# The gated delta rule's 64x64 triangular matrices, stored packed with two heads a tile and multiplied in the diagonal quarters of TensorE's array

## The chip, the core and the metric

The kernel runs on one core of one Trainium2 chip. The metric is the device time of the whole program in microseconds, here the median of three runs. A profile is taken of one further execution.

## What is computed

Two networks in a row on a sequence of 512 tokens, width 1024: a first one of two layers (a recurrent and gated-linear-attention mixer, then an attention with forgetting, called fox, each with an MLP) and a second one of two *hybrid* layers. A hybrid layer mixes with three things at once: sliding-window attention, sparse attention, and the gated delta rule. The change concerns the delta rule alone, four heads of width 128, chunks of 64 tokens:

```
q, k, v, g, beta = ...                       # per head; gc = cumsum(g) within a chunk of 64
decay = where(lower, exp(gc[:, None] - gc[None, :]), 0)
a_mat = where(strict, (k * beta) @ k.T * decay, 0)          # 64x64 for each chunk
rhs   = [v * beta, k * beta * exp(gc)]
u, w  = triangular_solve(a_mat + I, rhs)                    # unit lower triangular
qk    = where(lower, q @ k.T * decay, 0)                    # 64x64 for each chunk
for each chunk:                                             # 8 chunks, a scan
    v_new = u - w @ state
    o     = (q * exp(gc)) @ state + qk @ v_new
    state = state * exp(gc_last) + (k * exp(gc_last - gc)).T @ v_new
```

All arithmetic is float32.

## The kernel before

The program is written for the engines by hand, each engine with its own order of instructions and semaphores by name (`ev.mark` and `ev.at`). In a hybrid layer the attention and the delta rule share one stage. `paired_attention` goes through 34 slots `d`. In each it issues the two score products of slot d (L763, 64 contraction rows, one head in each row half), then the first delta step (`fill(d, 0)`), the products with the values of slot d-2 (L774, the two heads into the two column halves of a bank), the first transpose of the probabilities of slot d-1 (L788), the second delta step (`fill(d, 1)`) and the second transpose. VectorE takes the maxima (L1339), scales (L1362) and copies half the transposes (L1369); ScalarE takes the exponentials (L1916) and copies the other half (L1927). `STEPS` lays the list of `delta_steps` over the slots, two a slot, from slot 1 on.

The list has, for each pair of heads (0, 1) and (2, 3): rows, tok, kk of each head, then xt; then for each level k of 1 to 4 the step p for both heads and q for one and for the other; then p of level 5, last, and uw of each head. These are 23 steps for a pair. After both pairs come 16 steps of the scan over chunks (scan, kv).

The inverse of the unit triangular matrix is built by levels: X is the inverse so far, of blocks of 2^k, `XTM` its transpose, and `ATL` the transposed a_mat. A level takes the mask of its off-diagonal blocks (`level`, VectorE), p is their product with X (TensorE, L1007), ScalarE copies it to `PM` (L2190), q multiplies it with X from both sides (L1015 for X, L1018 for its transpose), and VectorE subtracts (L1630, L1632). The next p waits for the updates of the level before.

Each of these matrices stands in a tile of 128x512: 4 blocks of 128 tokens, each block a 128x128 matrix with two 64x64 chunks on its diagonal and zeros elsewhere. A product is a 128x128x128 product for each block. Each head of a pair has its own tiles, `gw(e, n)`, in `work_2` and `work`, and its own two banks, `ga(h)` and `gb_(h)`. `rows` broadcasts gc and a factor of beta over the partitions by a product with the identity (L971, L972), VectorE adds the mask of the decay (L1591) and multiplies k with beta (L1595), ScalarE takes the exponentials (L2170, L2171); `tok` transposes k and v (L982); `kk` forms k k^T and k q^T (L990, L991); `xt` transposes (L997); `uw` forms u and w (L1031, L1032). In the scan, chunk c of `qk` is read from rows and columns of its own 64x64 block (L1058).

The constants (masks, identity and tables) come in one DMA at the start, and TensorE waits for them before its first product.

## Time and profile before

| what | value |
|---|---|
| median of 3 runs | 3070.65 us (3068.67 to 3077.63) |
| the profiled execution's own time | 3068.48 us |
| its span on the core | 3067.0 us |
| mean granted TensorE clock | 0.956 of full (2.4 GHz) |
| TensorE, VectorE, ScalarE busy | 94%, 55%, 37% of the span |

Times in rows are microseconds from the start of the span; ns where it says so. PE is TensorE's products, PEld its weight loads, DVE VectorE, ACT ScalarE. The shapes of a product are its weights (rows*columns) and what it moves through them. The duration shown for one product contains its way through the array, so products overlap, and the pitch from start to start tells what one costs. A float32 product leaves two records. The granted clock is a share of 2.4 GHz: 1.00 is 2.4 GHz, 0.50 is 1.2 GHz.

### The profile page before, as it was taken

The page shows a single profiled execution, that of the slowest core. Times are in us where ns is not written, and L with a number is a line of the kernel's source. Part 1 is how long each engine was busy: PE and PEld are TensorE (multiplying, and loading weights), DVE is VectorE, ACT ScalarE, POOL GpSimd, SP SyncE. Part 2 cuts the span into 40 slices and gives each one's busy share as a digit, 9 for nine tenths or more (in the row PEclk, how much of TensorE's full clock was granted, in tenths as well). Part 3 has the DMA queues.
Part 4 walks back from the last instruction along what each step waited for, and adds up shares of the span by engine and source line. Part 5 has one row for each costly group of instructions (what it writes and reads, how often), then busy time and mean ns, then how long its engine had stood idle before and what let it go on. Part 6 is the DMA issues. An engine that isn't in the chain of part 4 may idle for free.

```text
span 3067.0 us, 35358 instructions
## 1 busy us (share of the span) xinstructions
PE 2870.2 (94%) x14106; PEld 2297.8 (75%) x14106; DVE 1673.6 (55%) x2910; ACT 1121.2 (37%) x1908; POOL 9.4 (0%) x21
## 2 busy tenths in 40 slices
PE   6878999999998999997998989999999999899998
PEld 4666888867666688884887767888868778678887
DVE  6748756563555665655546755444555477543334
ACT  3433423234554432424424443222334344332223
POOL 0000000000000000000000000000000000000000
PEclk9969999999998999998988999999999899999999
DMA  6324655532221365661230003444432100122222
GB/s 237 130 69 151 199 188 169 190 116 86 72 67 49 108 203 183 193 205 62 96 103 1 1 28 107 140 145 144 147 110 96 70 1 2 55 86 99 97 97 83
DMA packets 92067, 336.19 MB, mean 110 GB/s; under 512 B 10480, under 2 KB 10736, under 8 KB 91776
## 3 DMA queue, kind: packets, MB, share of 16 engines
q1 hardware_dynamic: 86800, 315.40, 31.1%
q10 hardware_dynamic: 3792, 14.31, 1.3%
q0 software_dynamic: 1312, 4.23, 0.5%
q8 instruction: 113, 1.85, 0.2%
q14 instruction: 50, 0.41, 0.0%
HBM read 331.76 MB, written 2.13 MB: 109 GB/s over the span
## 4 chain that ended last, share of the span: by engine, by line
PE 87%; DVE 7%; ACT 4%; DMA 1%; issue 1%; ACTq 0%; DVEq 0%
PE bank L595 22%; PE bank L596 22%; PE bank L597 22%; PE bank L774 2%; PE bank L788 2%; PE bank L763 2%; DVE in_low L1175 1%; DVE hidden L1178 1%; PE bank L1007 1%; PE bank L862 1%; PE bank L612 1%; PE bank L1015 1%; PE bank L613 1%; PE bank L614 1%; PE bank L643 1%
## 5 line engine op out<-in xcount | busy, mean ns | idle before, releaser
L595 PE MATMUL bank<-in_high,weights_high 128*128 128x512 f32 x2160 | 874.0, 405 | 45.8 <-DVE in_low L1175 34.5
L596 PE MATMUL bank<-in_low,weights_high 128*128 128x512 f32 x2160 | 856.0, 396 | 0.0
L597 PE MATMUL bank<-in_high,weights_low 128*128 128x512 f32 x2160 | 855.5, 396 | 0.0
L1085 DVE TENSOR_TENSOR weights_low<-weight_ring,weights_high 128x1024 fp32r<-128x1024 f32 x404 | 494.0, 1223 | 467.0 <-ACT weights_high L1710 467.0
L1710 ACT ACTIVATE weights_high<-weight_ring 128x1024 fp32r<-128x1024 f32 x404 | 424.6, 1051 | 482.7 <-PE bank L597 320.6
L595 PEld LDWEIGHTS bank<-in_high,weights_high 128*128 128x128 f32 x2160 | 414.3, 192 | 183.0 <-issue 55.4
L597 PEld LDWEIGHTS bank<-in_high,weights_low 128*128 128x128 f32 x2160 | 414.3, 192 | 88.9
L596 PEld LDWEIGHTS bank<-in_low,weights_high 128*128 128x128 f32 x2160 | 415.2, 192 | 85.3 <-issue 3.8
L595 PE MATMUL bank<-hidden_split,weights_high 128*128 128x512 f32 x864 | 336.2, 389 | 0.0
L597 PE MATMUL bank<-hidden_split,weights_low 128*128 128x512 f32 x864 | 336.2, 389 | 0.0
L596 PE MATMUL bank<-hidden_split,weights_high 128*128 128x512 f32 x864 | 336.2, 389 | 0.0
L1094 DVE CUSTOM_DVE_ANT_0 weight_ring<-weight_ring,silu_c,vectors 128x1024 f32<-128x1024 f32 x192 | 244.5, 1279 | 4.3 <-DMA weight_ring<-stream 4.2
L595 PEld LDWEIGHTS bank<-hidden_split,weights_high 128*128 128x128 f32 x864 | 162.2, 188 | 33.8
L597 PEld LDWEIGHTS bank<-hidden_split,weights_low 128*128 128x128 f32 x864 | 162.2, 188 | 33.7
L596 PEld LDWEIGHTS bank<-hidden_split,weights_high 128*128 128x128 f32 x864 | 162.2, 188 | 33.5
L1803 ACT ACTIVATE hidden_split<-tmp 128x512 fp32r<-128x512 f32 x108 | 68.4, 633 | 262.6 <-DVE tmp L1539 205.5
L1724 ACT ACTIVATE tmp<-bank 128x512 f32<-128x512 f32 (+1 forms) x77 | 45.9, 596 | 243.9 <-PE bank L597 243.9
L1916 ACT ACTIVATE probs<-probs,columns 128x256 f32<-128x256 f32 (+4 forms) x144 | 73.5, 512 | 165.5 <-DVE columns L1339 163.2
L1195 DVE TENSOR_TENSOR hidden_split<-tmp,hidden_split 128x512 fp32r<-128x512 f32 x108 | 74.8, 693 | 75.5 <-ACT hidden_split L1803 75.5
L1539 DVE TENSOR_TENSOR tmp<-bank,tmp 128x512 f32<-128x512 f32 x44 | 30.4, 691 | 118.3 <-PE bank L597 118.3
L1724 ACT ACTIVATE tmp<-bank,vectors 128x512 f32<-128x512 f32 (+1 forms) x65 | 44.6, 686 | 136.7 <-PE bank L597 136.7
L774 PE MATMUL bank<-probs_T,hidden 128*64 128x128 f32 (+1 forms) x816 | 70.6, 299 | 25.1 <-DVE probs_T L1369 25.1
(330 smaller groups left out, 2985.8 us busy)
## 6 DMA issues: line engine op xcount, KB each, us to landing
weight_ring<-stream SPq DMA_DIRECT2D x597, 512.0 KB, 3.4
mixer_out<-cmp ACTq DMA_DIRECT2D x6, 1024.0 KB, 4.8
hidden<-forget_rows POOLq DMA_DIRECT2D x16, 256.0 KB, 3.6
residual<-x ACTq DMA_DIRECT2D x4, 512.0 KB, 12.9
mixer_out<-cmp SPq DMA_DIRECT2D x2, 1024.0 KB, 5.9
out<-mixer_out ACTq DMA_DIRECT2D x4, 512.0 KB, 2.7
constants<-consts ACTq DMA_DIRECT2D x1, 2013.5 KB, 20.9
silu_c<-c ACTq DMA_DIRECT2D x2, 512.0 KB, 4.6
```

Source lines behind the costliest of these rows:

```text
L595: pe.matmul(bank[:, :], WHI[:, z, cols], high, start=(k == 0), stop=False)
L596: pe.matmul(bank[:, :], WHI[:, z, cols], low, start=False, stop=False)
L597: ins = pe.matmul(bank[:, :], WLO[:, z, cols], high, start=False, stop=(k == ktiles - 1))
L763: pe.matmul(B[2 + z][:, 0:w], it["q"], it["k"], start=True, stop=True).then_inc(*mark("tensor_attention", *name, "scores", 2 * d + z))
L774: ins = pe.matmul(it["out"], it["v"][c], turned[:, blk(c)], start=it["start"] and c == 0, stop=it["stop"] and c == m - 1, skip_group_check ...
L1085: v.tensor_tensor(WLO[:, z, :], ring[:, n % RING, :], WHI[:, z, :].bitcast(F32), ALU.subtract).then_inc(*mark("weights_low", "low", n))
L1094: v.tensor_tensor_reduce(w, w, SC[:, :], 1.0, vec1("ada_b", col, col + 1), ALU.mult, ALU.add, MODS[:, col:col + 1]).then_inc(*mark("modula ...
L1195: v.tensor_tensor(HSPLIT[:, 1, at_, :], tmp, HSPLIT[:, 0, at_, :].bitcast(F32), ALU.subtract).then_inc(*mark("vector_mlp", *event))
L1710: s.activation(WHI[:, i % NSPLIT, :], ring[:, n % RING, :], ACT.Copy).then_inc(*mark("weights_high", "high", n))
L1724: s.activation(dst, view(B_of(key)[:, :]), func, **kw).then_inc(*mark("scalar_evict", "evicted", key))
L1803: s.activation(HSPLIT[:, 0, at_, :], tmp, ACT.Copy).then_inc(*mark("scalar_mlp", *event))
L1916: s.activation(p, p, ACT.Exp, bias=nm, scale=-1.0, accum_out=COL[:, c + 2 + z:c + 3 + z]).then_inc(*mark(sem, *name, "exp", i))
```

## The change

- All 64x64 matrices are stored without their zeros. A packed matrix is 128 partitions x 256 columns: chunk 2b in partitions 0 to 63 and chunk 2b+1 in 64 to 127, both at columns 64b. Both heads of a pair share a tile of 512 columns (`pk(e, n)`), so operations that take a tile and a constant (level masks, the start of the inverse) run once for both heads, 512 wide. The others run once for each head, 256 wide.
- The products of xt, p, q and last are 64x64x64, two for each of before. Chunk z of a block is multiplied in the quarter of rows and columns of half z (`out64`, `half`), and successive products alternate between the two diagonal quarters, with different heads or different results, and so different banks. xt is a product with a 64x64 identity instead of a transpose.
- kk forms 128x64x64 products into both column halves.
- In rows, the broadcast of gc stays whole for the exponential `EG`; that of beta and a second one of gc are made packed. beta is multiplied onto the decay matrix (`PMB`) after its exponential, no longer onto k; tok waits for that.
- uw becomes two steps for the pair: step 0 takes chunk 0 of each block for u and chunk 1 for w, step 1 the other way round.
- p and last signal once for both heads. The mask for the next level waits for p of the level before.
- The scan reads `qk` at its packed place. The constants shrink: decay mask and identity 64 columns, six level masks 64 columns each, no `strict`.

The number of steps and their places in the slots stay. The core of the diff:

```diff
-                 ("rot", 128), ("band", 128), ("causal", 128), ("decay_mask", 128), ("strict", 128),
-                 ("levels", 6 * 128), ("gla_mask", 64), ("chunk_reset", T), ("cos", T), ("sin", T),
+                 ("rot", 128), ("band", 128), ("causal", 128), ("decay_mask", 64), ("ident64", 64),
+                 ("levels", 6 * 64), ("gla_mask", 64), ("chunk_reset", T), ("cos", T), ("sin", T),
...
-    level_mask = lambda e, k: M[:, 4 + 2 * e + k % 2, :]
+    pk = lambda e, n: U2[:, n, 256 * e:256 * e + 256]
+    pkb = lambda e, n, z, b: U2[half(z), n, 256 * e + 64 * b:256 * e + 64 * b + 64]
+    level_pair = lambda k: M[:, 4 + k % 2, :]
+    level_block = lambda e, k, z, b: M[half(z), 4 + k % 2, 256 * e + 64 * b:256 * e + 64 * b + 64]
+    out64 = lambda bank, z, b: bank[half(z), 64 * b:64 * b + 64]
...
-            out += [("p", hs, 5), ("last", hs)] + [("uw", h) for h in hs]
+            out += [("p", hs, 5), ("last", hs), ("uw", hs, 0), ("uw", hs, 1)]
...
-                    ins = pe.matmul(gb_(h)[:, blk(b)], c4(brow)[:, b, h:h + 1].broadcast_to([P, P]), ident,
-                                    start=True, stop=True)
+                for n, x in enumerate((brow, crow)):
+                    for b in range(NTB):
+                        for z in range(2):
+                            ins = pe.matmul(out64(gb_(h), z, NTB * n + b), c4(x)[:, b, h:h + 1].broadcast_to([P, 64]),
+                                            ident[:, half(z)], start=True, stop=True)
...
-                pe.wait_ge(*at("gdn_kbt", l, h))
+                pe.wait_ge(*at("gdn_pmb", l, h))
...
-                for b in range(NTB):
-                    pe.matmul(ga(h)[:, blk(b)], H[:, 4 + h, blk(b)], gw(e, KBT)[:, blk(b)], start=True, stop=True)
-                    ins = pe.matmul(gb_(h)[:, blk(b)], H[:, 4 + h, blk(b)], H[:, h, blk(b)], start=True, stop=True)
+                for bank, src in ((ga(h), 4 + h), (gb_(h), h)):
+                    for b in range(NTB):
+                        for z in range(2):
+                            ins = pe.matmul(out64(bank, z, b), H[:, 4 + h, chunk(2 * b + z)], H[:, src, chunk(2 * b + z)],
+                                            start=True, stop=True)
...
             elif name == "p":
                 hs, k = which
-                for e, h in enumerate(hs):
-                    pe.wait_ge(*at("gdn_mask", l, h, k))
+                pe.wait_ge(*at("gdn_mask", l, hs, k))
+                for h in hs:
                     pe.wait_ge(*at("gdn_xm", l, h, k))
                     if k > 1:
                         pe.wait_ge(*at("gdn_xtm_k", l, h, k - 1))
+                for turn_ in range(2):
                     for b in range(NTB):
-                        ins = pe.matmul(gb_(h)[:, blk(b)], level_mask(e, k)[:, blk(b)], gw(e, XM)[:, blk(b)],
-                                        start=True, stop=True)
-                    ins.then_inc(*mark("tensor_gdn", "gdn_p", l, h, k))
+                        for e, h in enumerate(hs):
+                            z = turn_ ^ e
+                            ins = pe.matmul(out64(gb_(h), z, b), level_block(e, k, z, b), pkb(e, XM, z, b),
+                                            start=True, stop=True)
+                ins.then_inc(*mark("tensor_gdn", "gdn_p", l, hs, k))
             elif name == "q":
...
-                for b in range(NTB):
-                    ins = pe.matmul(ga(h)[:, blk(b)], gw(e, XTM)[:, blk(b)], gw(e, PM)[:, blk(b)], start=True, stop=True)
+                for turn_ in range(2):
+                    for b in range(NTB):
+                        z = turn_
+                        pe.matmul(out64(ga(h), z, b), pkb(e, XTM, z, b), pkb(e, PM, z, b), start=True, stop=True)
+                        z = 1 - turn_
+                        ins = pe.matmul(out64(gb_(h), z, b), pkb(e, PM, z, b), pkb(e, XTM, z, b), start=True, stop=True)
...
             elif name == "uw":
-                h, = which
-                e = h % 2
-                pe.wait_ge(*at("gdn_xtm_k", l, h, 5))
-                for b in range(NTB):
-                    pe.matmul(ga(h)[:, blk(b)], gw(e, XTM)[:, blk(b)], gw(e, VBT)[:, blk(b)], start=True, stop=True)
-                    ins = pe.matmul(gb_(h)[:, blk(b)], gw(e, KBG)[:, blk(b)], gw(e, XTM)[:, blk(b)], start=True, stop=True)
-                ins.then_inc(*mark("tensor_gdn", "gdn_uwt", l, h))
+
+                hs, turn_ = which
+                for e, h in enumerate(hs):
+                    if turn_ == 0:
+                        pe.wait_ge(*at("gdn_xtm_k", l, h, 5))
+                    else:
+                        pe.wait_ge(*at("gdn_uw_half", l, h))
+                    for b in range(NTB):
+                        z = turn_
+                        pe.matmul(ga(h)[half(z), blk(b)], pkb(e, XTM, z, b), gw(e, VBT)[half(z), blk(b)], start=True, stop=True)
+                        z = 1 - turn_
+                        ins = pe.matmul(gb_(h)[:, chunk(2 * b + z)], gw(e, KBG)[half(z), blk(b)], pkb(e, XTM, z, b),
+                                        start=True, stop=True)
+                    ins.then_inc(*mark("tensor_gdn", "gdn_uwt" if turn_ else "gdn_uw_half", l, h))
...
-            def level(e, h, k):
-                v.tensor_tensor(r4(level_mask(e, k)), r4(gw(e, ATL)), over(lev[:, k * P:(k + 1) * P]), ALU.mult).then_inc(
-                    *mark(sem, "gdn_mask", l, h, k))
+            def level(hs, k):
+                v.tensor_tensor(r8(level_pair(k)), r8(U2[:, ATL, :]), over(lev[:, k * 64:(k + 1) * 64]), ALU.mult).then_inc(
+                    *mark(sem, "gdn_mask", l, hs, k))
...
+            def with_beta(e, h):
+                v.wait_ge(*at("gdn_pm", l, h))
+                v.tensor_tensor(pk(e, PMB), pk(e, PM), gb_(h)[:, 0:256], ALU.mult).then_inc(*mark(sem, "gdn_pmb", l, h))
...
-                v.tensor_tensor(gw(e, ATL), ga(h)[:, :], gw(e, PM), ALU.mult).then_inc(*step(sem))
-                v.wait_ge(*last(sem))
-                v.tensor_tensor(r4(gw(e, XM)), r4(gw(e, ATL)), over(lev[:, 0:P]), ALU.mult).then_inc(*step(sem))
-                v.wait_ge(*last(sem))
-                v.tensor_tensor(r4(gw(e, XTM)), over(ident), r4(gw(e, XM)), ALU.subtract).then_inc(
-                    *mark(sem, "gdn_xtm", l, h))
+                v.tensor_tensor(pk(e, ATL), ga(h)[:, 0:256], pk(e, PMB), ALU.mult).then_inc(*step(sem))
                 if e == 0:
                     inner(e, h)
+                else:
+                    v.wait_ge(*last(sem))
+                    v.tensor_tensor(r8(U2[:, XM, :]), r8(U2[:, ATL, :]), over(lev[:, 0:64]), ALU.mult).then_inc(*step(sem))
+                    v.wait_ge(*last(sem))
+                    v.tensor_tensor(r8(U2[:, XTM, :]), over(const("ident64")), r8(U2[:, XM, :]), ALU.subtract).then_inc(
+                        *mark(sem, "gdn_xtm", l, h))
+                    ev.also(sem, "gdn_xtm", l, h - 1)
+                    inner(e, h)
...
-                v.tensor_tensor(gw(e, XM), gw(e, XM), ga(h)[:, :], ALU.subtract).then_inc(*mark(sem, "gdn_xm", l, h, k + 1))
-                v.wait_ge(*at("gdn_qt", l, h, k))
-                v.tensor_tensor(gw(e, XTM), gw(e, XTM), gb_(h)[:, :], ALU.subtract).then_inc(*mark(sem, "gdn_xtm_k", l, h, k))
+                v.tensor_tensor(pk(e, XM), pk(e, XM), ga(h)[:, 0:256], ALU.subtract).then_inc(*mark(sem, "gdn_xm", l, h, k + 1))
+                v.tensor_tensor(pk(e, XTM), pk(e, XTM), gb_(h)[:, 0:256], ALU.subtract).then_inc(
+                    *mark(sem, "gdn_xtm_k", l, h, k))
...
-                s.activation(gw(e, PM), gw(e, PM), ACT.Exp).then_inc(*step(sem))
+                s.activation(pk(e, PM), pk(e, PM), ACT.Exp).then_inc(*mark(sem, "gdn_pm", l, h))
```

## Rows read from the trace of the kernel before

**Rows 1.** The page's first part: busy us (share of the span) xinstructions
```profile
PE 2870.2 (94%) x14106; PEld 2297.8 (75%) x14106; DVE 1673.6 (55%) x2910; ACT 1121.2 (37%) x1908; POOL 9.4 (0%) x21
```

**Rows 2.** Windows: stretch, its length, busy us of each engine, clock, DMA share
```profile
1646.40:1682.30 35.90, 35.74 (x296) 31.28 (x296) 28.32 (x86) 15.57 (x50) 0.00 (x0) 0.96 0.01 2
...
2467.00:2505.00 38.00, 37.89 (x321) 33.09 (x321) 29.81 (x91) 16.18 (x53) 0.00 (x0) 0.98 0.01 1
...
2514.00:2529.40 15.40, 12.00 (x98) 8.96 (x94) 13.10 (x39) 9.43 (x33) 0.00 (x0) 1.00 0.00 1
```

**Rows 3.** Timeline of TensorE over one level: start, duration, line, shapes, records
```profile
2483.72 1.95 PE L1007 MATMUL bank<-work,mixer_out 128*128 128x128 f32 x16
2485.51 0.38 PE L788 MATMUL bank<-constants,probs 128*128 128x128 f32 x2
2485.82 0.41 PE L763 MATMUL bank<-hidden 64*128 64x31 f32 x4
2486.16 1.16 PE L1015 MATMUL bank<-work 128*128 128x128 f32 x8
2487.16 1.06 PE L1018 MATMUL bank<-work 128*128 128x128 f32 x8
2488.14 0.66 PE L774 MATMUL bank<-probs_T,hidden 128*64 128x128 f32 x8
2488.73 0.44 PE L788 MATMUL bank<-constants,probs 128*128 128x128 f32 x2
2489.01 1.06 PE L1015 MATMUL bank<-work 128*128 128x128 f32 x8
2489.90 1.06 PE L1018 MATMUL bank<-work 128*128 128x128 f32 x8
2490.80 0.38 PE L788 MATMUL bank<-constants,hidden 128*128 128x128 f32 x2
...
2491.53 2.05 PE L1007 MATMUL bank<-work,mixer_out 128*128 128x128 f32 x16
```

**Rows 4.** Groups by line, TensorE, whole span: busy us, mean ns, idle before
```profile
L1007 PE MATMUL bank<-work,mixer_out 128*128 128x128 f32 x320 | 42.9, 291 | 3.0 <-ACT work L2185 1.7 <-DVE mixer_out L1581 1.3
L1015 PE MATMUL bank<-work 128*128 128x128 f32 x256 | 36.1, 284 | 0.6 <-ACT work L2190 0.4
```

**Rows 5.** Timeline of TensorE, products in parts of the array
```profile
187.38 2.28 PE L717 MATMUL bank<-hidden 64*64 64x64 f32 x58 [11.38 <-ACT hidden L1890]
...
189.78 2.92 PE L726 MATMUL bank<-hidden 64*64 64x128 f32 x60
...
1608.54 0.24 PE L923 MATMUL bank<-probs_T 128*64 128x31 f32 x1
...
1608.74 0.22 PE L925 MATMUL bank<-probs_T 128*64 128x31 f32 x1
```

**Rows 6.** Windows on the granted clock, with quarters (187 to 192) and with gaps
```profile
187.40:188.40 1.00, 1.00 (x28) 1.00 (x30) 0.00 (x0) 0.00 (x0) 0.00 (x0) 0.50 0.10 41
...
191.40:192.40 1.00, 1.00 (x34) 1.00 (x28) 0.00 (x0) 0.00 (x0) 0.00 (x0) 0.78 0.00 0
...
966.00:969.00 3.00, 2.12 (x10) 1.49 (x10) 2.57 (x7) 1.77 (x5) 0.00 (x0) 0.50 0.00 0
```

**Rows 7.** Timeline of the same level, ScalarE and VectorE
```profile
2484.82 0.60 ACT L2190 ACTIVATE work<-bank 128x512 f32<-128x512 f32 x1 [0.51 <-PE bank L1007]
...
2486.32 0.42 DVE L1369 COPY probs_T<-bank 128x256 f32<-128x256 f32 x1
...
2491.00 0.69 DVE L1632 TENSOR_TENSOR work<-work,bank 128x512 f32<-128x512 f32 x1 [0.20 <-PE bank L1018]
```

**Rows 8.** Timeline of TensorE in the scan, wide weights with 64 moving columns
```profile
2576.59 1.11 PE L1046 MATMUL bank<-hidden,work 128*128 128x64 f32 x8
2577.63 0.44 PE L774 MATMUL bank<-probs_T,hidden 128*64 128x128 f32 x4
```

**Rows 9.** The page's DMA issues: KB each, us from issue to landing
```profile
constants<-consts ACTq DMA_DIRECT2D x1, 2013.5 KB, 20.9
```

88 lines of the change are left out of this document (49 added, 39 removed).

## The prediction

> **What bounds the kernel now.** I read the page first: TensorE is busy for 94% of the span [rows 1]. That is an average over many stages, so I next read the windows of the only stage the change touches, the one in each hybrid layer where attention and the delta rule share the engines. It starts at about 1615 and 2434 us and lasts some 194 us each time. Its two inversion loops per layer are where the change works, and there TensorE has work for 35.7 of 35.9 us and for 37.9 of 38.0 us at a granted clock of 0.96 and 0.98, while VectorE shows 28 to 30 us and ScalarE 16 us [rows 2]. So TensorE sets the pace of the loops. Between them (the row from 2514 us) it has 12.0 of 15.4 us: here the chain through VectorE and ScalarE counts as well [rows 2]. Then the timeline of one level of the inversion [rows 3]: p from 2483.72 to 2485.51 (1.79 us for 16 records, 112 ns each), q of one head 2486.16 to 2488.14, q of the other 2489.01 to 2490.80, next p at 2491.53. One level takes 7.81 us, of which the delta products are 1.79 + 1.98 + 1.79 = 5.56 and attention's pieces between them 2.25. It fills one and a half slots of the interleaving (5.2 us each). Every float32 product leaves two records, so the 320 and 256 records of p and of one half of q are 160 and 128 products [rows 4].
>
> **What a small product costs.** The trace of before has no product in a quarter at the full clock, so I bound it. A whole 128x128 product is 2 x 112 ns. Two products whose outputs lie in different column halves do overlap: attention's L774, 128 moving columns, has 8 records between 2488.14 and 2488.73, and less some 0.17 us of issue gap that is 0.42 us or 53 ns a record, half of 112 [rows 3]. The compression's pairs with 31 columns come at 1608.54 to 1608.74 for eight records, 29 ns each [rows 5]. Products in true quarters stand only in the first layer, at clock 0.50: 58 records with 64 columns in 2.28 us (39 ns each) and 60 records with 128 columns in 2.92 us (49 ns) [rows 5]; at 1.2 GHz that is more overlap than two. In the change only two quarters alternate (rows and columns 0 to 63, rows and columns 64 to 127), each with half the columns of before: half of 53 is 27 ns. My bounds are 27 and 39 ns, and I take 28, near the pair of column halves at the full clock. The Trainium skill, TensorE: Matmul & The Clock Gate, Part 1, says that starts never come closer than about 25 ns; the 29 ns of the eight records do not contradict it, and by 25 ns the sum would gain some 6 us.
>
> Changing between a whole array and a part costs something too: L1015 right after L763 takes 1.00 us to its successor, after L788 0.89, so 0.1 us; L774 to L788 shows 0.17 [rows 3].
>
> **The change part by part.** All counts are for both layers: four pairs of heads, four levels each with a p and two q, then a fifth p and "last".
> - *Levels, 16 of them.* p is 32 records in place of 16, as is each q: 3 x 32 x 28 ns = 2.69 us. A step in the second half of a slot stands between transposes on the whole array and now pays two changes (0.27 us); one and a half steps of each level do: 0.4. With attention's 2.25 and the 0.1 after L763 that makes 5.44 us on TensorE. VectorE's work shrinks as well: four updates of 0.69 us [rows 7] become 256 columns wide, for which the copy of 256 columns from a bank at 0.42 is the nearest row [rows 7]; two masks of 0.69 become one. The mask moves ahead and waits for the product before last, off the path. But what is late next is the loop through the engines: after the second q come two updates (0.84) before p may start. Today p at 2491.53 starts while the last update of the other head still runs (2491.00 plus 0.69) [rows 7]; afterwards it waits for both heads in one go, with 0.7 us of attention on TensorE as cover. ScalarE's copy (0.60 for 512 columns today [rows 7], less for 256) has the L774 and L788 pieces as cover, unless the exponentials stand ahead of it in ScalarE's order. I put 0.3 us a slot for these stalls (bounds 0 and 1), 0.45 a level. 7.81 - 5.89 = 1.9; times 16, **30 us**.
> - *Fifth p and "last", four of each.* 3.58 to 1.8 plus changes and a stall: 1.3 us saved a pair, **5 us**.
> - *kk and xt.* kk's 16 records of 112 ns become 32 of half a width, into two column halves: 0.9 us less a head, 0.75 after the changes of tiling, 6 us over eight heads. The masked start (two operations of 0.69) is done once for both heads, and the pair's chain to the first p gets shorter by about that. On the other side p waits for both copies, and head 1 pays the joint operations. 0.75 us a pair: **9 us** in all (bounds 4 and 16, since 3.4 us of TensorE's window are idle [rows 2]).
> - *rows and tok.* One of two broadcasts becomes 32 short records, 0.9 us as before; VectorE's product with beta moves behind ScalarE's exponential, and tok waits for it. VectorE and TensorE both have the next head's step queued behind; the exponential starts without waiting for VectorE now. I take 0, bounds -2 and +4 us.
> - *uw.* This is where it pays back. 64-row operands give two products for each of before: 128 moving columns against 64 columns of weights, or 64 moving columns against 128 of weights. With 128 columns of weights a product with 64 moving ones is no cheaper: L1046 has 8 records between 2576.59 and 2577.63, at least 108 ns each after the gap [rows 8]. So a pair has 64 records of 112 ns, 7.2 us for 3.6 before, if they run one after another: 3.6 x 4 = **14 us lost**. They alternate between the row halves; overlapped by two, nothing is lost.
> - *The constants* shrink by 512 of some 4000 columns, a quarter of a megabyte of 2013.5 KB [rows 9]; at the same rate, less than 2.6 of the 20.9 us, and they share the engines with the weights. I take 0.6 us saved.
> - The scan reads its 64-wide blocks from another place and costs the same: 0.
>
> Sum: 30 + 5 + 9 - 14 + 0.6 = **31 us**. Against the profiled execution's own 3068.5 that is 3037.5, against the median of the runs (3070.65, 2.2 us above it) 3039.6. I say **3038 us**. The stage has full weight buffers and no DMA to speak of, so what it saves the end gets.
>
> **Rivals.**
> 1. *Everything overlaps.* uw's row halves run side by side (14 us back) and the stalls are hidden (7 us back): 3017. For it: L717 and L726 overlap at half clock more than I assume [rows 5].
> 2. *uw drains the array at each product.* Its products alternate between two shapes of tile, which no row of before does; by the 0.1 us of a change in [rows 3], eight products in each of 16 head turns add 13 us: 3051. The Trainium skill, TensorEngine Tiling, Key Properties, says that changing the tiling mode, not just the tile, drains the engine; that is this rival, and the 0.1 and 0.17 us agree with its direction.
> 3. *The loop is bound by latency.* The stalls are 1 us a slot, not 0.3: 16 x 1.05 = 17 us less gain, 3055. For it: four engine changes for each level; against it: attention's pieces fill them.
> 4. *The clock.* With 2.12 of 3.00 us of work TensorE ran at 0.50 near the end of the first network's attention [rows 6]. At half clock a level has at least 2 x 2.69 us of quarters and some 5 of attention and changes, 10.4 in place of 5.9: 72 us over all levels. It turns the gain into a loss once 43% of the loops' levels run so. At half of them, 3074. Against it: quarter products raised the clock, from 0.50 at 187.40 to 0.78 at 191.40 with nothing but quarters between [rows 6].
> 5. *The quarters don't overlap* (the change doesn't do what it says). About 2048 records lie in p, q, last and kk. Each ns of pitch is 2 us, and the gain is gone at 28 + 15 = 43 ns. At 53 ns p costs 1.7 us and the levels, the fifth p and "last" save nothing; uw's 14 us and some 3 us of added changes stay, against 3 us of joint VectorE operations and 0.6 of constants: 3068.5 + 17 - 3.6 = **3082, slower**. Against it: L717's 39 ns at half the clock.
> 6. The stage is bound by something that the change doesn't touch: 3068. The busy rows speak against it [rows 2].
>
> **How the numbers follow.** Forecast with its own spread, 3025 to 3046: 0.42. Rival 1: 0.18; 2: 0.12; 3: 0.10; 4: 0.07; 5: 0.07; 6: 0.04. The measurement can tell about 0.3% (9 us) from no change, so faster means below 3061.4: the first four, 0.82, less a little for the ends, 0.81. Same takes rival 6 and half of rival 4, 0.08; slower rival 5 and the other half, 0.11. The range 3006 to 3062 leaves out rivals 4 to 6 and the far tail of rival 1; it reaches 39 ns pitch (22 us less gain, 3060) and, below, uw overlapped, no stalls and kk with xt at their bound (28 us more, 3010).
>
> **What would show it.** Right: p's 32 records within 0.8 to 1.1 us, a slot of 3.7 to 4.2 us in the loops where it was 5.2, VectorE's share up, uw's steps of about 3.6 us each, clock at 1. Wrong: records 53 ns apart (5), uw steps of 5 us (2) or 1.8 (1), waits of TensorE for the updates or for ScalarE's copy near 1 us a slot (3), stretches of clock 0.50 in the loops (4). The two hybrid layers should save alike, within a microsecond or two.

## The result, and the profile after

| | before | after |
|---|---|---|
| median of four runs each | 3069.66 us (3068.64 to 3077.63) | 3136.38 us (3124.60 to 3140.22) |
| the profiled execution, its span | 3068.48, 3067.0 us | 3136.84, 3135.4 us |
| mean granted clock | 0.956 | 0.930 |

The change makes the kernel slower: ratio 1.0205, 95% interval 1.0173 to 1.0237. The forecast was 3038 us, faster. Here and below a ratio compares only the runs within 1.5% of the fastest run of their kernel; medians and ranges take in all runs.

The page of the kernel after, its line on TensorE's busy time (us, share, instructions) and its slices (each digit a fortieth of the span, busy tenths and granted clock):
```profile
PE 2934.0 (94%) x15546; PEld 2320.0 (74%) x15546; DVE 1627.0 (52%) x2882; ACT 1109.0 (35%) x1908; POOL 9.4 (0%) x21
...
PE   5879999999998999989989999999999899999998
...
PEclk9979999999998999999988679999999985899999
```
TensorE is as busy as before [rows 1], but in two places, slices 23 and 24 and again 33 to 35 (counted from 1), the clock is at 6, 7, 8, 5 and 8 tenths. They take in the second half of the delta rule of each hybrid layer: slices 23 and 24 are 1724 to 1881 us, 33 to 35 are 2508 to 2743 us.

The loops did what was forecast. This is the timeline of TensorE over one level in the second layer (start, duration, line, shapes, records). L1029 is p, L1039 and L1041 are the two results of q, and L784 and L798 are attention's:
```profile
2496.63 1.15 PE L1029 MATMUL bank<-work,mixer_out 64*64 64x64 f32 x32 [0.65 <-ACT work L2226]
2497.71 0.44 PE L798 MATMUL bank<-constants,hidden 128*128 128x128 f32 x2
...
2499.57 0.22 PE L1041 MATMUL bank<-work 64*64 64x64 f32 x1
2499.58 0.22 PE L1039 MATMUL bank<-work 64*64 64x64 f32 x1
2499.63 0.22 PE L1041 MATMUL bank<-work 64*64 64x64 f32 x1
2499.64 0.22 PE L1039 MATMUL bank<-work 64*64 64x64 f32 x1
2499.79 0.66 PE L784 MATMUL bank<-probs_T,hidden 128*64 128x128 f32 x8
...
2502.75 1.15 PE L1029 MATMUL bank<-work,mixer_out 64*64 64x64 f32 x32
```
p takes 1.08 us to its successor where it took 1.79 [rows 3]. Two records of q start every 0.058 us, which makes 29 ns each, and the two of such a pair, in different quarters, start within 0.01 us of each other. The level is 6.1 us long, where the one read before took 7.8 [rows 3].

The same timeline at the first uw steps of that layer (L1062 is u, 64x64 of weights; L1064 is w, 64x128 of weights; one product is two records):
```profile
2524.55 0.43 PE L1062 MATMUL bank<-work 64*64 64x128 f32 x2
2524.91 0.43 PE L1064 MATMUL bank<-work 64*128 64x64 f32 x2
2525.28 0.43 PE L1062 MATMUL bank<-work 64*64 64x128 f32 x2
...
2527.72 0.68 PE L1062 MATMUL bank<-work,work 64*64 64x128 f32 x2
2528.33 0.68 PE L1064 MATMUL bank<-work,work 64*128 64x64 f32 x2
```
Every product starts 0.36 us after the one before it, and after eight of them the distance is 0.61 us. No row of this step names a wait or another engine: the products themselves are slow. Windows of that layer (stretch, length, busy us and records of PE, PEld, DVE, ACT, POOL, then the granted clock and DMA):
```profile
2496.60:2510.00 13.40, 12.90 (x261) 9.96 (x263) 11.44 (x41) 7.04 (x27) 0.00 (x0) 1.00 0.01 2
...
2530.00:2540.00 10.00, 10.00 (x35) 5.98 (x34) 2.01 (x9) 1.89 (x6) 0.00 (x0) 0.50 0.01 2
...
2560.00:2570.00 10.00, 8.26 (x166) 6.31 (x166) 9.29 (x27) 4.35 (x14) 0.00 (x0) 1.00 0.01 2
...
2640.00:2650.00 10.00, 10.00 (x42) 7.70 (x41) 3.96 (x9) 2.59 (x7) 0.00 (x0) 0.50 0.00 0
```
The loops (first and third row) run at 1.00, that is 2.4 GHz. In the uw steps (second row) and in the scan (fourth) the clock is 0.50, 1.2 GHz. The view shows TensorE busy for 10.00 of 10 us there, with 35 records: busy time is a sum of overlapping durations, and longer records fill it as well as more of them. The record count beside it is what gives the stretch away.

The scan's own product with w, all records of one layer (ns min/median/max, first and last start), before and then after:
```profile
L1041 PE MATMUL bank<-work,work x64: 272/273/324, 2575.6 to 2618.0; 128*64 128x128 f32 x64
```
```profile
L1074 PE MATMUL bank<-work,work x64: 272/421/475, 2615.2 to 2687.2; 128*64 128x128 f32 x64
```
The same instructions take 72 us from first to last in place of 42, with a median of 421 ns in place of 273.

The stages can now be laid side by side. The lengths come from the starts of the first and last records of each step. The last column is a kernel told of below, which has everything packed but u and w.

| us, first / second hybrid layer | before | after | u, w full size |
|---|---|---|---|
| rows to first p | 26.8 / 26.9 | 21.8 / 20.7 | 21.8 / 22.0 |
| first p to first "last" (the loop, heads 0, 1) | 35.8 / 35.9 | 26.2 / 26.2 | 26.2 / 26.2 |
| to the end of the second pair's fifth p | 65.3 / 65.3 | 71.3 / 71.2 | 55.3 / 56.4 |
| to the scan's first product | 8.8 / 8.8 | 22.7 / 21.2 | 8.9 / 8.9 |
| scan, first product to last | 45.4 / 45.4 | 78.1 / 75.0 | 45.4 / 45.4 |
| sum | 182.1 / 182.3 | 220.1 / 214.3 | 157.6 / 158.9 |

After against before, this is 38.0 + 32.0 = 70 us; the spans differ by 68.4.

### The profile page after: what moved, and what is told of

The parts are those of the page before. It is cut to its first block, busy times and chain, and to the rows that moved or that the text cites. A ratio compares the mean times of both kernels' runs of the same rounds, so it can differ in the third digit from the quotient of the medians.

```text
span 3135.4 us, 38214 instructions
## 1 busy us (share of the span) xinstructions
PE 2934.0 (94%) x15546; PEld 2320.0 (74%) x15546; DVE 1627.0 (52%) x2882; ACT 1109.0 (35%) x1908; POOL 9.4 (0%) x21
## 4 chain that ended last, share of the span: by engine, by line
PE 87%; DVE 7%; ACT 4%; DMA 1%; issue 1%; ACTq 0%; DVEq 0%
PE bank L605 22%; PE bank L606 21%; PE bank L607 21%; PE bank L773 2%; PE bank L798 2%; PE bank L784 2%; PE bank L1064 1%; PE bank L1062 1%; DVE in_low L1208 1%; DVE hidden L1211 1%; PE bank L872 1%; PE bank L622 1%; PE bank L1074 1%; PE bank L623 1%; PE bank L624 1%; PE bank L653 1%
## 5 line engine op out<-in xcount | busy, mean ns | idle before, releaser
L1843 ACT ACTIVATE hidden_split<-tmp 128x512 fp32r<-128x512 f32 x108 | 68.4, 633 | 262.7 <-DVE tmp L1572 205.9
L784 PE MATMUL bank<-probs_T,hidden 128*64 128x128 f32 (+1 forms) x816 | 75.9, 316 | 24.2 <-DVE probs_T L1402 24.2
```

The source lines that it names most:

```text
L784: ins = pe.matmul(it["out"], it["v"][c], turned[:, blk(c)], start=it["start"] and c == 0, stop=it["stop"] and c == m - 1, skip_group_check ...
L1843: s.activation(HSPLIT[:, 0, at_, :], tmp, ACT.Copy).then_inc(*mark("scalar_mlp", *event))
```

## The experiments

The theory at the outset was that the alternating shapes of u's and w's products empty the array at each change, and that the half clock in uw and scan is a consequence of that. The rivals were that the half clock belongs to the scan, to the packed layout or to the pairing of the two row halves.

**The products of a step grouped by shape.** All eight 64x64 products of both heads first, in alternating diagonal quarters, then all eight 64x128 ones, in alternating row halves.
```diff
-                for e, h in enumerate(hs):
...
-                    for b in range(NTB):
-                        z = turn_
+                for h in hs:
+                    pe.wait_ge(*(at("gdn_uw_half", l, h) if turn_ else at("gdn_xtm_k", l, h, 5)))
+                for b in range(NTB):
+                    for e, h in enumerate(hs):
+                        z = turn_ ^ e
                         pe.matmul(ga(h)[half(z), blk(b)], pkb(e, XTM, z, b), gw(e, VBT)[half(z), blk(b)], start=True, stop=True)
-                        z = 1 - turn_
+                for b in range(NTB):
+                    for e, h in enumerate(hs):
+                        z = 1 - turn_ ^ e
                         ins = pe.matmul(gb_(h)[:, chunk(2 * b + z)], gw(e, KBG)[half(z), blk(b)], pkb(e, XTM, z, b),
...
+                event = "gdn_uwt" if turn_ else "gdn_uw_half"
+                ins.then_inc(*mark("tensor_gdn", event, l, hs[0]))
+                ev.also("tensor_gdn", event, l, hs[1])
```


> The changed kernel with the products of uw in another order: in each step first all eight 64x64 products for u, the two heads in the two diagonal quarters in turn, then all eight 64x128 products for w, the two heads in the two row halves in turn. Theory A (changing the tile's shape at every product drains the array, and the thin work drops the clock, which the scan then keeps): a step falls from 5.8 us to about 2 us (32 records, pairs overlapping, 54 to 60 ns each), the clock stays at 1.00 through uw and the scan, the scan's span falls from 82 to about 52 us a layer, and the whole to 3136 - 2 x 57 = about 3022 us. Rival B (the row halves can't run side by side with 64-row operands, whatever the order): a step takes 3.6 us and the whole is about 3036. Rival C (the clock falls because the loops before leave TensorE too little work, not because of uw): uw gets shorter, the scan stays at 0.50, the whole is about 3085.

Measured: median 3077.71 us of ten runs, from 3035.36 to 3091.23; ratio to the kernel before on that chip (3069.99) 0.9961, interval 0.9915 to 1.0007, so no difference is shown; the medians themselves stand at 1.0025. Timeline, first of its steps in the second layer, then the scan's start:
```profile
2552.63 0.27 PE L1060 MATMUL bank<-work 64*64 64x128 f32 x1
2552.67 0.27 PE L1060 MATMUL bank<-work,work 64*64 64x128 f32 x1
2552.74 0.27 PE L1060 MATMUL bank<-work 64*64 64x128 f32 x1
2552.78 0.27 PE L1060 MATMUL bank<-work,work 64*64 64x128 f32 x1
...
2559.57 1.94 PE L1076 MATMUL bank<-work,work 128*64 128x128 f32 x8 [1.36 <-ACT work L2240]
```
A record of each head starts every 0.11 us, so a product costs about 0.11 us on average and a step of 16 takes 2.06 us with its one change of shape (2552.50 to 2554.56) in place of 5.8. The clock stays at 1.00 through uw. But TensorE then waits 1.36 us for ScalarE's copies of u and w, which here come for both heads at the end, and the scan of the profiled run is at half the clock all the same, for 44 us of the second layer and 65 of the first:
```profile
2550.00:2558.00 8.00, 7.42 (x112) 5.93 (x111) 2.87 (x15) 2.11 (x9) 0.00 (x0) 1.00 0.01 3
...
2568.00:2578.00 10.00, 10.00 (x43) 7.96 (x43) 4.58 (x13) 2.38 (x7) 0.00 (x0) 0.50 0.01 2
```
Two of the ten runs, 3035 and 3038 us, have a mean clock of 0.957 and 0.956 where the others have 0.935 to 0.946. The shapes cost what was thought; the scan's clock is a second matter, and it is not decided by the uw steps' clock alone. So the steps came out as theory A has them, but none of the ten runs reached its 3022; most lie near rival C's 3085, though the clock of 1.00 up to the end of uw speaks against rival C's cause.

**Twenty-four full products between uw and scan.** The changed kernel, with this ahead of the scan:
```diff
                 if c == 0:
                     pe.wait_ge(*at("gdn_uw", l, 3))
+                    for n in range(24):
+                        pe.matmul(B[0][:, 0:P], ident, ident, start=True, stop=True)
```


> The changed kernel with 24 whole 128x128x128 products of the identity with itself (48 records) ahead of the scan's first product, into a bank that the scan then overwrites; uw stays as it is. Theory A (the scan's own work can't raise the clock from 0.50, and would keep it at 1.00): the clock rises within the added work of some 8 us a layer, the scan takes about 52 us in place of 82, and the whole falls by 2 x (30 - 8) = 44 us to about 3092. Rival C2 (the scan's work in the changed kernel drops the clock by itself): the scan returns to 0.50 within some 10 us, and the whole rises by up to 16 us to 3150.

Measured: 3113.19 us, one run. Windows of the scan of the first layer (two rows) and of the second:
```profile
1764.00:1774.00 10.00, 10.00 (x83) 8.66 (x81) 4.67 (x14) 2.03 (x7) 0.00 (x0) 1.00 0.01 2
...
1780.00:1820.00 40.00, 40.00 (x180) 32.49 (x179) 16.15 (x45) 6.63 (x20) 0.00 (x0) 0.50 0.00 0
...
2620.00:2660.00 40.00, 40.00 (x325) 32.52 (x324) 28.94 (x82) 13.07 (x40) 0.00 (x0) 1.00 0.00 1
```
The clock came back in both layers. In the second it stayed, and 40 us of scan hold 325 records; in the first it fell again in the middle of the scan, and 40 us hold 180. So the half clock is not only handed over from uw: a scan that started at 1.00 fell later by itself. The time lies between the two that were expected, with one layer as each of them has it.

**The kernel before, with u and w in alternating half products.** Nothing packed, no pairing of heads.
```diff
-                for b in range(NTB):
-                    pe.matmul(ga(h)[:, blk(b)], gw(e, XTM)[:, blk(b)], gw(e, VBT)[:, blk(b)], start=True, stop=True)
-                    ins = pe.matmul(gb_(h)[:, blk(b)], gw(e, KBG)[:, blk(b)], gw(e, XTM)[:, blk(b)], start=True, stop=True)
+                for turn_ in range(2):
+                    for b in range(NTB):
+                        z = turn_
+                        hz = slice(64 * z, 64 * z + 64)
+                        pe.matmul(ga(h)[hz, blk(b)], gw(e, XTM)[hz, chunk(2 * b + z)], gw(e, VBT)[hz, blk(b)], start=True, stop=True)
+                        z = 1 - turn_
+                        hz = slice(64 * z, 64 * z + 64)
+                        ins = pe.matmul(gb_(h)[:, chunk(2 * b + z)], gw(e, KBG)[hz, blk(b)], gw(e, XTM)[hz, chunk(2 * b + z)], start=True, stop=True)
...
```


> The kernel before, with uw alone done as in the change: two products of 64 contraction rows for each of before, a 64x64 one and a 64x128 one in turn, on the unpacked matrices. Theory A: each product takes 0.36 us at the full clock and 0.61 at half, so uw goes from 1.8 us a head to 6 to 10, 2 x 4 x 6 = some 45 us in all, the clock falls to 0.50 in the second pair's uw and stays there over the scan, 60 us more: about 3170 us. Rival C (the thinner loops are needed for the fall of the clock): uw costs 32 us and the scan keeps 1.00: about 3103.

Measured: 3131.65 us, one run, 62 more than the kernel before. Windows of the second layer: its loop, for comparison, then its second pair's uw steps and the scan's start:
```profile
2530.00:2540.00 10.00, 9.94 (x77) 7.89 (x75) 4.84 (x19) 3.27 (x12) 0.00 (x0) 1.00 0.01 2
...
2620.00:2630.00 10.00, 9.94 (x37) 6.02 (x36) 0.08 (x1) 1.31 (x3) 0.00 (x0) 0.53 0.00 0
2630.00:2640.00 10.00, 9.94 (x35) 6.54 (x35) 1.41 (x6) 2.18 (x6) 0.00 (x0) 0.50 0.01 2
2640.00:2650.00 10.00, 10.00 (x76) 8.20 (x74) 7.40 (x20) 2.78 (x9) 0.00 (x0) 0.94 0.00 0
```
The alternation brings the clock down in the unpacked kernel too, in all four uw places. So neither the packed layout nor the pairs of heads are needed for it. But here the scan left the half clock within 3 us of its start in both layers and stayed at 1.00, which is why the time is under theory A's 3170; it is over rival C's 3103 because the clock fell in uw.

**The kernel before, with a pause of 6 us ahead of the scan.** Twelve clears in a row on VectorE, each waiting for the one before, hold back the scan's first state.
```diff
+                    for n in range(12):
+                        v.memset(state[0], 0.0).then_inc(*step(sem))
+                        v.wait_ge(*last(sem))
                     v.memset(state[0], 0.0).then_inc(*mark(sem, "scan_state", l, 0))
```


> The kernel before, with VectorE clearing the scan's state twelve more times, one after the other, ahead of the scan, so that TensorE stands still for some 6 us in each hybrid layer; no product is changed. Theory A (the scan keeps the clock that it finds): the clock falls to 0.50 in the pause and stays there for most of the scan, so the loss is 2 x (6 + about 28) = 68 us: about 3138. Rival D (the scan raises the clock by itself, as the broadcasts of rows do at the stage's start, within 6 us): the loss is 2 x (6 + 3) = 18 us: about 3088.

Measured: 3096.02 us, one run. The clock was 0.50 from the pause until some 10 us into the scan, then 1.00:
```profile
2593.00:2608.00 15.00, 10.69 (x46) 8.70 (x47) 7.84 (x24) 1.98 (x7) 0.00 (x0) 0.50 0.00 0
...
2612.00:2622.00 10.00, 10.00 (x84) 8.13 (x84) 7.27 (x22) 4.01 (x13) 0.00 (x0) 1.00 0.01 2
```
This refutes that the scan always keeps the clock that it finds (3138); the rival with 3088 was nearer.

**All packed but u and w.** The last subtraction writes X^T into a full-size tile whose blocks off the diagonal were cleared once a layer (two tiles of `work` that packing had left free), and uw is what it was before. With that each head has a step of its own again, and ScalarE copies its u and w as soon as they are ready.
```diff
+    full = lambda e: U[:, 1 + 2 * e, :]
...
-                    v.tensor_tensor(pk(e, XTM), pk(e, XTM), gb_(h)[:, 0:256], ALU.subtract).then_inc(
-                        *mark(sem, "gdn_xtm_k", l, h, 5))
+                    for z in range(2):
+                        v.tensor_tensor(r4(full(e))[half(z), :, half(z)], r4(pk(e, XTM))[half(z)],
+                                        r4(gb_(h)[:, 0:256])[half(z)], ALU.subtract).then_inc(
+                                            *(mark(sem, "gdn_xtm_k", l, h, 5) if z else step(sem)))
...
+                if k == 2 and hs[0] == 0:
+                    for e in range(2):
+                        v.memset(full(e), 0.0).then_inc(*step(sem))
...
+                h = hs[turn_]
+                pe.wait_ge(*at("gdn_xtm_k", l, h, 5))
+                for b in range(NTB):
+                    pe.matmul(ga(h)[:, blk(b)], full(turn_)[:, blk(b)], gw(turn_, VBT)[:, blk(b)], start=True, stop=True)
+                    ins = pe.matmul(gb_(h)[:, blk(b)], gw(turn_, KBG)[:, blk(b)], full(turn_)[:, blk(b)], start=True, stop=True)
+                ins.then_inc(*mark("tensor_gdn", "gdn_uwt", l, h))
...
+                h = hs[turn_]
+                s.wait_ge(*at("gdn_uwt", l, h))
+                s.activation(H[:, UT + h, :], ga(h)[:, :], ACT.Copy).then_inc(*step(sem))
+                s.activation(wt(l, h), gb_(h)[:, :], ACT.Copy).then_inc(*mark(sem, "gdn_uw", l, h))
```


> The changed kernel, with one part undone: the last product's subtraction on VectorE writes each head's X^T into a 512-column tile whose blocks off the diagonal were cleared once a layer, and u and w are again the 16 products of 128x128 a head that the kernel before had, each head in a step of its own and copied by ScalarE as soon as it is ready. All else stays packed. It adds four half-height subtractions and takes two away per pair, and two clears a layer: under 2 us a layer on VectorE. Theory A (all that the change loses, the alternating tile shapes of uw and the half clock in uw and scan, comes from the uw steps): uw is back at about 3.6 us a pair, the granted clock is 1.00 through uw and through the scan, and what the loops saved remains, some 25 us a layer less two or three: 3070 - 2 x 23 = 3024 us, between 3015 and 3035. Theory B (the packed kernel's scan or loops leave the array too thin, whatever uw does, so that the clock falls to 0.50 at the scan's start as it did with the grouped products): about 3070 us, with 0.50 over some 45 us of each scan. Theory C (the gain of the loops is smaller than read, because a stage behind takes it back): 3035 to 3060 with the clock at 1.00.

Measured: median 3018.21 us of four runs (3016.16 to 3019.60); ratio to the kernel before on that chip 0.9826, interval 0.9790 to 0.9861. Timeline of its uw, then windows of its uw and its scan, second layer:
```profile
2520.03 0.39 PE L1060 MATMUL bank<-work,work 128*128 128x128 f32 x2
2520.25 0.39 PE L1059 MATMUL bank<-work,work 128*128 128x128 f32 x2
```
```profile
2519.70:2525.00 5.30, 5.21 (x42) 4.34 (x42) 2.81 (x14) 2.71 (x9) 0.00 (x0) 1.00 0.00 0
2525.00:2571.00 46.00, 45.57 (x362) 36.55 (x362) 33.28 (x96) 16.95 (x51) 0.00 (x0) 1.00 0.01 1
```
A product that does twice the work costs 0.22 us against 0.36. The scan takes 45.4 us in both layers, to a tenth what it took before. Theory A holds in all its parts, and the time is 6 us under its 3024. This kernel beats both others: its median is 118 us under that of the kernel after (116 by the two ratios), and it is some 53 under the kernel before by the ratio. The stretch from the fifth p to the scan, which holds the half-height operations that it adds on VectorE, takes 8.9 us where the kernel before takes 8.8.

**The same with the pause of 6 us.** One run, and later more runs of the same kernel and of the kernel before with its pause; the edit is the one above.

> The kernel with full-size u and w, and 12 extra clears in a row on VectorE ahead of the first state of the scan, the same pause of about 6 us that was put into the kernel before. There the clock fell to 0.50 in the pause and was back at 1.00 some 10 us into the scan, and the kernel lost 26 us. If the packed kernel's scan is the same work for the clock (theory A), this kernel shows the same: 0.50 for 10 to 20 us around each scan's start, then 1.00, and about 26 us more than the one without the pause. If the packed kernel's scan holds the half clock that it finds (theory B: something that packing left thinner in the scan or beside it), 0.50 lasts for most of each scan, and it costs 50 to 70 us more.

> The kernel before with the 6 us pause ahead of each scan, now several times, to see the spread of what a scan does that starts at the half clock. Theory S (the scan can stay at the half clock or leave it, whichever kernel it stands in, and small differences in its start decide): times spread from 3090 to 3130 us. Theory K (the kernel before's scan always leaves it within 17 us): all within 3090 to 3102.

> The kernel with full-size u and w and the same pause, several times: the packed kernel's counterpart. One look gave 3060 us, 42 above its own kernel without the pause, with two or three low stretches a layer. Theory S: spread from 3043 to 3085 us, about the same distances above its own kernel as in the kernel before with the pause. Theory K (what packing left in the scan makes it hold the half clock longer): its distances above its own kernel are 15 us or more larger than those of the kernel before with the pause, in every run.

Measured: the first run took 3060.43 us, 42 more than without the pause, between the two that were expected. Then came ten runs from 3047.79 to 3073.46, median 3051.88, and four runs of the kernel before with the pause, from 3095.44 to 3126.28, median 3098.67. Above their own kernels without a pause that is 30 to 55 us, median 34, and 24 to 55, median 27. In the slowest of the ten, which is the profiled one, the clock is at 0.50 for 65 us of the second layer; in the first layer it comes back, falls again and comes back:
```profile
1750.00:1755.00 5.00, 5.00 (x37) 4.13 (x37) 3.88 (x9) 0.87 (x3) 0.00 (x0) 0.84 0.00 0
1755.00:1765.00 10.00, 10.00 (x48) 8.45 (x48) 3.71 (x13) 2.00 (x7) 0.00 (x0) 0.50 0.00 0
1770.00:1780.00 10.00, 10.00 (x81) 8.24 (x80) 7.23 (x23) 3.34 (x12) 0.00 (x0) 1.00 0.00 0
```
Theory S fits: a scan that is disturbed at its start has no fixed clock. The two profiles of this same kernel differ in the second layer: in one the scan is at 0.50 for 12 us, at 1.00 for 3 and at 0.50 for 14 more, in the other at 0.50 for 65 us without a break. For the kernel before this rests on times alone, one run of 3126 us with a mean clock of 0.944 beside three of 3095 to 3100 with 0.950 to 0.952; the slow one has no profile. Theory K, that packing made the scan hold the half clock longer, would put every packed run 15 us or more further out; the medians differ by 6. So small a difference is not excluded.

**The order within a step, two more ways.** First, for each head its four 64x64 products and then its four 64x128 ones, no head interleaved:
```diff
                     for b in range(NTB):
                         z = turn_
                         pe.matmul(ga(h)[half(z), blk(b)], pkb(e, XTM, z, b), gw(e, VBT)[half(z), blk(b)], start=True, stop=True)
+                    for b in range(NTB):
                         z = 1 - turn_
                         ins = pe.matmul(gb_(h)[:, chunk(2 * b + z)], gw(e, KBG)[half(z), blk(b)], pkb(e, XTM, z, b), start=True, stop=True)
```


> The changed kernel with the products of each uw step in another order only: for each head first its four 64x64 products, then its four 64x128 ones, no head interleaved with the other. Each head's products of a kind lie in the same rows of the array, so nothing runs in the other half beside them. Theory 1 (what costs is the change of tile shape between successive products, 32 times a pair in the changed kernel, 8 times here): a step of 16 products of 0.11 or 0.055 us and four changes of 0.3, 1.3 us + 1.2 = 2.5 us against 5.8 in the changed kernel, and near the 2.1 to 2.4 of the kernel in which both heads' products were interleaved. Theory 2 (what costs is that a product waits for the one before it in the same rows, whatever its shape): the step stays at 4 to 6 us, since here all products of a group share their rows. The time is near 3075 under theory 1, with the spread that the grouped kernel had, 3035 to 3091, and near 3130 under theory 2.

Second, the changed kernel's order, with the 64x128 product in the same row half as the 64x64 one before it:
```diff
-                        z = 1 - turn_
                         ins = pe.matmul(gb_(h)[:, chunk(2 * b + z)], gw(e, KBG)[half(z), blk(b)], pkb(e, XTM, z, b), start=True, stop=True)
```


> The changed kernel with one line less: in each uw step the 64x128 product takes the same half of the array's rows as the 64x64 product before it, where the changed kernel gives it the other half; the shapes alternate as before. It tells the change of shape from the change of rows. Theory 1 (the change of shape costs): at full clock a product still starts 0.36 us after the one before it, a step takes 5.8 us, and the kernel's time is the changed kernel's, 3125 to 3140 us. Theory 2 (the change of rows costs, and products that stay in their rows run at the 0.25 us that the serial kernel showed): 0.25 us a product, 4 us a step, and a time of 3080 to 3110 us.

Measured: 3083.31 and 3111.76 us, one run each. Timeline of the serial kernel's uw of heads 2 and 3 in the second layer, then a window of it:
```profile
2546.04 1.08 PE L1062 MATMUL bank<-work 64*64 64x128 f32 x8
2547.06 1.10 PE L1065 MATMUL bank<-work 64*128 64x64 f32 x8
2548.09 1.57 PE L1062 MATMUL bank<-work,work 64*64 64x128 f32 x8
...
2552.51 1.97 PE L1062 MATMUL bank<-work 64*64 64x128 f32 x8
2554.41 1.97 PE L1065 MATMUL bank<-work 64*128 64x64 f32 x8
```
```profile
2549.00:2556.00 7.00, 7.00 (x33) 5.67 (x31) 0.00 (x0) 0.28 (x1) 0.00 (x0) 0.50 0.01 2
```
Timeline of the first step of the kernel with the same rows:
```profile
1668.74 0.43 PE L1062 MATMUL bank<-work 64*64 64x128 f32 x2
1669.10 0.43 PE L1063 MATMUL bank<-work 64*128 64x64 f32 x2
1669.46 0.43 PE L1062 MATMUL bank<-work 64*64 64x128 f32 x2
```
In the serial kernel one head takes 2.05 us for eight products, 0.26 each. My 2.5 us a step was wrong: 4.1 is what it takes at full clock, since these products, which share their rows and, four at a time, their bank, don't overlap. Which of the two holds them apart was not tested; the grouped kernel alternates both. The kernel with the same rows but changing shapes shows 0.36 us, as the changed kernel does. Theory 1 of its expectation holds for the pitch, though its 3112 us lie under the range: its scans take 65.6 and 60.8 us where the changed kernel's take 78.1 and 75.0.

The serial kernel shows one thing more. Its clock fell to 0.50 in three of its four uw places too, and right behind the fourth, though its shape changes only after every fourth product. In the rows above this comes 2 us after the first product, and four products take 1.90 us at the end where they took 1.02 at the start. Only the grouped order and the full-size products kept 1.00 through every uw. So a change of shape at each product is not needed for the fall; which property of the slower orders brings it is not shown.

At 2.4 GHz, a product of 64 rows costs:

| order of u's and w's products | us a product |
|---|---|
| shape changes each time, other row half (after) | 0.36 |
| shape changes each time, same row half | 0.36 |
| shape stays, same row half (serial) | 0.26 |
| shape stays, row halves in turn (grouped) | 0.11, 0.13 with the one change |
| for comparison, whole array, twice the work a product (before) | 0.22 |

**Full-size u and w for one pair of heads only.** The edit above, for heads 0 and 1, or for heads 2 and 3.

> The changed kernel with the full-size u and w products for heads 0 and 1 only; heads 2 and 3, whose products stand right ahead of the scan, keep the packed ones with their alternating shapes. Theory (the loss has two parts, the uw steps' own time and the half clock that the scan starts with): only the first pair's part is recovered, some 12 us a layer, and the scan still runs at 0.50 for most of its length. Against the kernel with all at full size, 3018 us: plus 2 x (11.6 - 3.6 at full clock, some 8 more for the half clock, 28 to 32 in the scan), 3018 + 2 x 46 = 3110 us, between 3095 and 3120. Rival (each pair's low clock is a loss of its own, and the scan's is the sum of what both left behind): about 3075.

> The opposite: packed u and w products for heads 0 and 1, full-size ones for heads 2 and 3. Theory (the loss has two parts): the clock falls to 0.50 in the first pair's uw and comes back in the preludes and loops of the second pair, as it did in the changed kernel; the scan runs at 1.00. 3018 + 2 x (8 of alternation at full clock + 4 to 8 of half clock) = 3042 to 3050 us. Rival (a low clock left from the first pair's uw carries further): over 3065, with 0.50 in the second pair's loops.

Measured: with the first pair full, median 3073.54 us of eight runs, from 3042.15 to 3106.60; with the second pair full 3056.64 of eight, from 3046.94 to 3063.58. Windows, the first kernel's scans of both layers, and then the second kernel's scan of the second layer:
```profile
1730.00:1785.00 55.00, 55.00 (x226) 41.53 (x225) 19.28 (x57) 12.19 (x36) 0.00 (x0) 0.50 0.00 1
...
2590.00:2630.00 40.00, 40.00 (x320) 31.84 (x317) 28.80 (x82) 15.13 (x45) 0.00 (x0) 1.00 0.00 1
```
```profile
2564.00:2576.00 12.00, 11.47 (x90) 9.12 (x88) 8.78 (x26) 5.04 (x15) 0.00 (x0) 1.00 0.01 1
2576.00:2588.00 12.00, 12.00 (x55) 9.26 (x54) 4.46 (x15) 2.17 (x8) 0.00 (x0) 0.51 0.00 0
```
The first expectation, 3095 to 3120, was missed by six of the eight runs. The slow uw steps right ahead of the scan make the half clock likely there, not certain: in the profiled run one scan takes 78.1 us and the other, with the clock back at 1.00 within 2 us of its start, 46.3. The second, 3042 to 3050, was too low, for a reason that neither theory had: with full-size products right ahead and some 11 us of scan at 1.00 behind them, the clock still fell for 13 to 14 us, in both layers. The placement of the loss is as expected, the sizes are not.

## Why the prediction was wrong

*Levels, fifth p and last: right.* The forecast was 30 + 5 = 35 us. In the kernel with full-size u and w the loop of the first pair takes 26.2 us for 35.8, and that of the second, from first p to first "last", 29.6 for 38.1 (first layer): 9.6 + 8.5, 36 us over both layers. The pitch was forecast at 28 ns and is 29. The 25 ns between starts that the prediction names bind no single pair here, as the two records of a pair start within 0.01 us of each other; the mean lies above them. Inside, the sizes were off in both directions, so that a sum within 1 us is in part luck. The level I read took 7.8 us, but the four of the first pair average 8.39 and become 6.06, and those of the second go from 8.89 to 6.89, so 16 of them save some 35 us; the fifth p with "last" saves some 2, not 5. One sign went the other way: VectorE's share did not rise, it was 79% in the first loop of the kernel before and is 78% in that of the kernel after, since its work shrank with the loop.

*kk, xt, rows and tok: right within bounds.* The forecast was 9 us with bounds 4 and 16. The first pair's prelude saves 5.0 us and the second's 0.9, some 12 in two layers.

*The constants: 0.6 us.* TensorE's first product starts at 25.03 us (after) and 23.87 us (full-size u and w) where it started at 25.32. The first hybrid layer's rows start 2.9 and 2.6 us earlier; how much of that is the constants' is not shown.

*uw: this step failed, by its size.* The sum has -14 us, from 64 records a pair at 112 ns one after another. The serial kernel shows that this was nearly the price of that case (128 to 130 ns a record). What wasn't in the sum is that the diff's products change their shape each time. A product costs 0.36 us for 0.22 of the full-size one that does twice its work: 32 x 0.36 - 16 x 0.22 = 8 us a pair, 32 us for both layers at the full clock alone. Rival 2 had this and priced it nearly right. Its 0.1 us a change from [rows 3] is what the runs show, 0.36 with the shape changing against 0.26 with it kept in the same rows; its 14 + 13 = 27 us lost stand against 32, and its step of 5 us against 16 x 0.36 = 5.8. But the steps of the changed kernel really took 6.0 to 9.8 us, because the clock fell in or before them, and that no part of the prediction had. The Trainium skill, TensorEngine Tiling, Key Properties, says that changing the tiling mode, not just the tile, drains the engine. The 0.36 us whatever the rows, and the 0.11 where only the tile alternates, agree with that.

*The clock: the step left out, and the larger part.* "The scan [...] costs the same: 0" failed: it was wrong by 62 us. Another 24 lie around the uw steps: after minus full-size is 55.6 us from the rows to the scan's start, of which 32 are the shapes at full clock, and 62.3 in the scan. The 24 are a remainder that I put down to the half clock, which lasts some 20 us from each first pair's uw on and 13 to 17 from the second pair's uw to the scan. That is 118 us in all, where I had 14. Rival 4 had the half clock, but in the loops, where the changed kernel's profile doesn't show it, and my argument against it (quarters raised the clock [rows 6]) was about those. I asked what the new products do to the clock only for p and q, not for the steps whose pace I had as slowest, and did not ask what runs next. The Trainium skill, TensorE: Matmul & The Clock Gate, Part 1, ties the clock to how busy the engine has been lately. This case's traces do not show what is counted: the busy time of the view is 10.00 of 10 us in uw at 0.50, with 35 records, and 9.94 of 10 at 1.00, with 77 records, in the unpacked kernel's loop shown above (2530 to 2540).

*Without uw the forecast holds.* The rest of the sum was 31 + 14 = 45 us. The full-size kernel saves 24.5 + 23.4 = 48 us in the two stages, and 52.7 between the profiled spans. The 5 us over come half ahead of the first hybrid stage and half behind the last; their cause stays open.

*Left open.* It is not known what decides whether a scan leaves the half clock or falls to it. Undisturbed, the kernels before and with full-size u and w kept 1.00 through all four scans that were profiled. After a disturbance the same scan showed low stretches of 2 to 65 us in packed and unpacked kernels, also with nothing slow right ahead of it. The length of the disturbance does not order them: 17 us of half clock in the pause kernels, some 20 in the unpacked alternating one, a wait of 1.36 us in the grouped one, whose scan was low for 44 and 65. The grouped kernel differs from the full-size one in two things, the products of uw and the later copies by ScalarE with that wait. No run has the grouped products with early copies, or the full-size ones with late copies, so which of the two its scan's clock hangs on is not shown.

## What to carry to other kernels

- Packing small matrices pays if products of one shape follow each other and alternate between tiles, as p and q do here. Where operands on either side keep 128 columns, unpack them at the last moment (two half-height operations on VectorE here) rather than mix 64x64 and 64x128 tiles: that was the difference between 2% slower and 1.7% faster.
- Where a change slows TensorE's pace anywhere, price that stage and the one behind it at half the clock as a rival: here the half clock was some 86 of the 118 us. In windows read record counts beside the busy time. Where the clock is in play one run says little: take several.


## What the runs showed of the hardware

- Float32 products of 64 rows, 64x64 or 64x128, at 2.4 GHz: 0.36 us each when the shape changes at every product, 0.26 us when it stays, in the same rows and the same bank, 0.11 us when it stays and the row halves and the banks alternate. At 1.2 GHz the changing ones start 0.61 us apart.
- Quarter products in the two diagonal quarters with 64 moving columns start 29 ns a record apart on average at 2.4 GHz, two of different quarters within 0.01 us of each other.
- The granted clock fell after 8 to 15 products at 0.36 us in the four uw places of the changed kernel, after ten in the kernel with the same rows (first layer) and after eight at 0.26 us in the serial one (second pair, second layer), with no wait of the engine among them. It stayed at 1.00 through products at 0.11 us and through full-size ones at 0.22.
- A scan ran at 0.50 for up to 65 us without a break with the profile showing 100% busy. Runs of one program differ by up to 64 us (3042 to 3107, first pair full; 3035 to 3091, grouped), and their mean clocks go with it (0.958 to 0.933; 0.957 to 0.935).
